# Two hand-overs in the query and key loop change places: when banks return to the queue, and when VectorE empties the transposes

## What is computed

```python
q = (rms_norm_2(q_lat, q_a_norm) @ w_qb).reshape(b, s, 8, 96)
kv = (rms_norm_2(kv_lat, kv_a_norm) @ w_kvb).reshape(b, s, 8, 128)
k_nope, v = kv[..., :64], kv[..., 64:]
k = jnp.concatenate([k_nope, k_pe], axis=-1)
q = rms_norm_2(q, q_norm)
k = rms_norm_2(k, k_norm)
q = jnp.concatenate([q[..., :64], apply_rope(q[..., 64:], pos)], axis=-1)
k = jnp.concatenate([k[..., :64], apply_rope(k[..., 64:], pos)], axis=-1)
# softmax(q k^T) v per block of 128 queries, causal
```

## Time and profile before

| | us |
|---|---|
| median of 3 runs | 1593.05 |
| lowest, highest | 1591.18, 1593.5 |
| the profiled execution | 1595.3 |
| its span, first to last instruction | 1593.5 |
| its mean granted TensorE clock | 0.967 of full |

### The profile page before, as it was taken

The page is one execution under the profiler, slowest core; times in us unless marked ns, Lnnn a source line. Parts: engine busy times, 40 slices in busy tenths (PEclk is TensorE's granted clock), DMA queues, the critical chain, the costliest instruction groups (busy, mean ns, idle before and its releaser), DMA issues.

```text
span 1593.5 us, 23667 instructions
## 1 busy us (share of the span) xinstructions
PE 1487.3 (93%) x10032; PEld 1152.6 (72%) x10032; DVE 799.6 (50%) x1257; ACT 585.6 (37%) x1017; POOL 312.2 (20%) x257
## 2 busy tenths in 40 slices
PE   5999898998899999999998999989899899998989
PEld 3777676876688888888876787767687577776667
DVE  7766785444533323324346555546643556454652
ACT  4256341445332222223323443334433343333531
POOL 0000233101011101100003323533300333343420
PEclk8999899998899999999989999999999999999999
DMA  9239243601132222232220122212122112111122
GB/s 362 73 109 110 89 175 132 214 29 51 57 102 95 93 93 93 97 132 95 93 94 30 61 69 67 64 42 67 53 93 100 40 53 80 53 67 53 53 69 90
DMA packets 51368, 143.11 MB, mean 90 GB/s; under 512 B 13248, under 2 KB 17984, under 8 KB 50496
## 3 DMA queue, kind: packets, MB, share of 16 engines
q1 hardware_dynamic: 51264, 141.60, 28.1%
HBM read 136.90 MB, written 4.69 MB: 89 GB/s over the span
## 4 chain that ended last, share of the span: by engine, by line
PE 80%; DVE 10%; ACT 4%; issue 3%; POOL 2%; DMA 1%; SPq 0%; DVEq 0%; POOLq 0%; ACTq 0%
PE b L407 78%; ACT arena L2207 3%; POOL arena L2867 2%; PE b L410 2%; DVE arena L1267 2%; DVE arena L1275 2%; DVE ringr L1267 1%; DVE arena L1973 1%; DVE arena L2164 1%; ACT ring L2210 1%; DVE arena L1271 1%; DMA cst<-in_cst 1%; DVE tile L1267 1%; DVE arena L1278 1%; POOL arena L2870 0%
## 5 line engine op out<-in xcount | busy, mean ns | idle before, releaser
L407 PE MATMUL b<-tile,ring 128*128 128x512 f32 (+1 forms) x1840 | 664.2, 400 | 8.3 <-ACT tile L2210 8.0
L407 PEld LDWEIGHTS b<-tile,ring 128*128 128x128 f32 (+1 forms) x1840 | 349.0, 190 | 95.6 <-issue 15.4
L407 PE MATMUL b<-HR,ring 128*128 128x512 f32 (+1 forms) x944 | 388.1, 411 | 24.1 <-DVE arena L1267 13.8
L1267 DVE TENSOR_TENSOR ringr<-ring,ring 128x1024 fp32r<-128x1024 f32 x186 | 240.6, 1298 | 317.0 <-ACT ring L2210 315.9
L407 PE MATMUL b<-HR,ringr 128*128 128x512 f32 (+1 forms) x944 | 373.4, 396 | 0.0
L407 PE MATMUL b<-arena 64*64 64x64 f32 (+10 forms) x3104 | 235.4, 279 | 34.8 <-DVE arena L1278 16.2
L2210 ACT ACTIVATE ring<-ring 128x1024 fp32r<-128x1024 f32 x186 | 195.3, 1054 | 163.2 <-DMA ring<-in_ws 163.2
L407 PEld LDWEIGHTS b<-HR,ring 128*128 128x128 f32 (+1 forms) x944 | 179.4, 190 | 73.2 <-issue 16.6
L407 PEld LDWEIGHTS b<-arena 64*64 64x64 f32 (+5 forms) x3104 | 149.3, 142 | 111.6 <-issue 87.7
L407 PEld LDWEIGHTS b<-HR,ringr 128*128 128x128 f32 (+1 forms) x944 | 179.4, 190 | 45.9
L407 PE MATMUL b<-tile,ringr 128*128 128x512 f32 x448 | 179.5, 401 | 0.0
(11 more groups left out here) (131 smaller groups left out, 1261.3 us busy)
## 6 DMA issues: line engine op xcount, KB each, us to landing
ring<-in_ws SPq DMA_DIRECT2D x218, 512.0 KB, 3.5
arena<-in_ws SPq DMA_DIRECT2D x15, 512.0 KB, 15.2
arena<-in_lw SPq DMA_DIRECT2D x2, 1280.0 KB, 6.0
X<-in_xT SPq DMA_DIRECT2D x2, 1024.0 KB, 6.2
arena<-scr_kpad SPq DMA_DIRECT2D x8, 256.0 KB, 11.4
X<-in_xT SPq DMA_DIRECT2D x1, 2048.0 KB, 11.6
outT<-X SPq DMA_DIRECT2D x8, 256.0 KB, 2.0
arena<-in_cst SPq DMA_DIRECT2D x1, 1088.0 KB, 6.0
```

Source lines behind the costliest of these rows:

```text
L407: return self.e.matmul(out, lhsT, rhs, start=start, stop=stop, skip_group_check=True)
L1267: return self.e.tensor_tensor(out=out, in0=a, in1=b, op=op)
```

## The change

TensorE's program gives the banks of queries and keys back after the transposes of the block before, instead of ahead of them. VectorE's program empties the transposes of the block before right after it has multiplied queries and keys, ahead of its wait for GpSimd and of the two instructions of the rotation.

```diff
 # Tensor.qk
             self.give((l, "v", q), (act, (l, "v", q)))
             yield
+            yield
+            if q:
+                transposes(q - 1)
             for hh in range(2):
                 self.give((l, "q", q, hh), (dve, (l, "q", q, hh)))
             self.give((l, "k", q), (dve, (l, "k", q)), (act, (l, "sqk", q)))
-            yield
-            if q:
-                transposes(q - 1)
             yield
 # Vector.qk
             self.tt(kq[:, 0, :, 0:64], h64(k.bank[l, "k", q]), bc(s_[:, 0], 64), ALU.mult).then_inc(*dve.inc((l, "k", q)))
             yield
+            if q:
+                transposes(q - 1)
             x1, x2 = kq[:, :, :, 64:80], kq[:, :, :, 80:96]
             self.wait_ge(pool, (l, "rot", q))
             self.tt(x1, k.T4[:, 0], k.T4[:, 1], ALU.subtract).then_inc(*dve.inc((l, "rot1", q)))
             self.tt(x2, k.T4[:, 2], k.T4[:, 3], ALU.add).then_inc(*dve.inc((l, "rot", q)))
-            if q:
-                transposes(q - 1)
             yield
```

## The result

The changed kernel took 1612.22 us (median of 4 runs, 1610.35 to 1612.73) against 1592.12 us before (median of 4, 1590.99 to 1593.5): a ratio of 1.0124 with a 95% interval from 1.0106 to 1.0141, slower by 20.1 us. The forecast was 1608.0, in a range from 1602 to 1613. The profiled execution is the fastest of the four, 1610.35 us with a span of 1608.6, 15.1 us more than the 1593.5 of before.

What follows compares the result with a forecast made beforehand. TensorE bounds the kernel, its six dense tiles waiting for VectorE's multiplications. Added stall 10.3 us plus clock 4.65 makes 14.95 on the profiled 1595.3, 1610.25; that execution lies 2.25 above the median, so 1608.0 us, range 1602 to 1613.

Steps and rivals of the forecast that it cites:

- What bounds: Dense tiles of blocks 1 to 3, both layers: TensorE waits 2.08 or 2.76 us for VectorE's first multiplication, on the path.
- Part 1, other banks: Dense tile gets the bank of a transpose instead of queries' first half, so it waits for VectorE's eviction.
- Part 2, 1.71 us a stall: Eviction follows the three multiplications, so each of six dense tiles starts 1.71 us later, 10.3 us in all.
- Part 3, the cover: Evictions fit VectorE's idle time before GpSimd's products end; rotation not later, split 1.4 us earlier, gain not passed on.
- Part 4, the clock: Longer stalls make all six dense tiles slow: three more clock drops of 1.55 us, 4.65 us.
- The bound of 2.6 us: Upper clock loss per dense tile, from the stretch after a 4.05 us idle time; 11 us more for all six.
- Sum: 10.3 + 4.65 = 14.95 us on the profiled execution, giving 1610.25 us; median expected at 1608.0 us.
- constant 2.25 us: How far the profiled execution lies above the median, used to go from 1610.25 to 1608.0 us.
- Only the stall: Rival: idle times before dense tiles grow, but clock drops no more often or costs little; 1603.4 us, 10%.
- Stretched evictions: Rival: GpSimd's products slow VectorE's evictions beside them, TensorE waits 1.4 us more six times; 1616.5 us, 4%.
- No change: Rival: weights, not the bank, end the dense tile's wait, so the bank wouldn't matter; 1593 us, 4%.
- faster: Rival: VectorE's queue delays the next block's sums, so earlier evictions gain up to 8.4 us; 1584.6 us, 2%.

Runs made afterwards that it cites:

- e7: Kernel before with the never-returned eighth bank given back to the queue at the start of the first hybrid layer: 1579.43 us, ratio 0.9927.
- e8: Kernel before with the eighth bank returned to the queue and VectorE's half of the change: 1572.66 us, ratio 0.9884.
- e1: Kernel before with TensorE's half of the change alone, VectorE's program left as it was: 1629.72 us, ratio 1.0239.
- e9: Changed kernel, both halves, with the eighth bank returned to the queue: 1572.31 us, ratio 0.9863 against the kernel before.
- e3: Kernel before with 8 useless matmuls put into each of the six TensorE stalls: 1589.45 us, ratio 0.9981.
- e4: Changed kernel with 14 useless matmuls put into each of the six TensorE stalls: 1600.77 us, ratio 1.004 against the kernel before.
- e2: Kernel before with VectorE's half of the change alone, banks given back as before: 1592.84 us, ratio 1.0001.
- the fillers: Useless matmuls put into the six stalls: 8 each in the kernel before, 1589.45 us; 14 each in the changed kernel, 1600.77 us.
- e5_after_again: Changed kernel unaltered, run again for a second profile: 1613.41 us, ratio 1.0138 against the kernel before.

## Why the prediction held, point by point

**What bounds.** Right. The six dense tiles stood on the path, and what released them was the first multiplication; taking that wait away gives 12.7 us (`e7`), and 19.5 with VectorE's half as well (`e8`).

**Part 1, other banks.** Right, and shown by `e1` and `e9`: the same order of give calls costs 36.8 us with VectorE's old order and 20.1 with its new one while there are seven banks, and nothing with eight and the new order.

**Part 2, 1.71 us a stall.** Right. Stalls of 3.79 and 4.48 us where 3.79 and 4.47 were worked out, 24.1 us in all for 24.1; 3.43 us for two between `e3` and `e4`.

**Part 3, the cover.** Right: the rotation still ends after GpSimd's products, nobody waits for the split, and `e2` is within 0.13% of the kernel before. What this part says of VectorE's gain, that it isn't passed on, holds only while TensorE stalls; `e7` and `e8` show it passed on once the stall is gone.

**Part 4, the clock.** This is the term that was mis-sized. That all six tiles would be slow was right, in both profiles. But 1.55 us was taken for each, and the two behind the 4.48 us stalls cost 2.5 to 2.8 us. The bound of 2.6 us had been worked out from the stretch behind the 4.05 us idle time and was put aside with the reason that the tiles are the same work. That reason failed: the same 24 matmuls last 7.2 or 8.4 us, by whether the clock falls inside the tile or is low already at its start. The term is 6.7 and 7.1 us in the profiles where 4.65 were forecast, and about 7.9 by the fillers. The length of the idle time alone doesn't give the price either: behind idle times of 6.87 us the tiles of `e1` cost 2.0 to 2.3 us, less than those behind 4.48. What else sets it stays open.

A second weak place is that the sum was made on one execution's share of drops and carried over to the median by a constant 2.25 us. The share changes from one execution to the next: `e2`, with the same stalls of TensorE, has two slow tiles in its profile (37.09 us for the six) where the kernel before had three. Whether a typical run of the kernel before pays 3.5 us of clock or 4.65 the medians can't say.

**Sum.** The median came out 4.2 us above the forecast 1608.0. For the profiled execution 1610.25 us were worked out and 1610.35 measured, and that close a hit is luck. Its stalls grew by 10.3 us and its tiles by 6.7, 2.1 more than forecast, but it reached the end of block 0's transposes, up to which the two programs do the same, 2.3 us earlier (848.37 for 850.66). Of the 20.1 us between the medians 10.3 are stall and 6.7 to 7.9 clock, together 17.0 to 18.2. The interval of the 20.1 us goes from 16.9 to 22.4, so the rest may be noise. Some 0.5 us of it shows in both profiles after, between the last dense tile of the first layer and the first stall of the second (355.26 and 355.45 us for 354.79); what it comes from wasn't traced.

**Rivals.** Only the stall: out, the clock's share grew by 6.7 us or more. Stretched evictions: out, 0.73 us beside GpSimd's products. No change and faster: out with these banks. The mechanism of the faster rival, VectorE's queue as the bound, turned up in `e7`, where its condition (no idle time ahead of the sums) is met.

## What to carry to other kernels

Where buffers are handed out first in, first out, the order of the give calls is a table of waits: before moving one, write down for every later take whose emptying it inherits, and what stands ahead of that in the emptying engine's queue. A consumer on the critical path should get the buffer that has been empty longest, and a buffer that was taken and never returned is worth looking for: here it was worth 12.7 us alone and 19.5 us together with the change's VectorE half. A stall on TensorE costs its own length and then some of the clock: here 1.5 to 2.8 us for each of the 18 stalls of 3.79 us or more.

## What was not expected of the hardware

The price of a clock drop is not one number, and it doesn't simply grow with the idle time. The same 24 matmuls last 5.67 us at full clock, 7.2 us behind those idle times of 2.08 to 3.80 us that brought the clock down, and 8.15 to 8.44 us behind 4.46 to 4.48 us (four cases). But in `e1_tensor_half` they last 7.67 to 7.98 us behind 6.86 and 6.87 us (four cases), and 8.30 and 8.48 behind 7.54 and 7.55. What goes with the price is where the clock fell. In all tiles of 7.2 us the first matmul takes 0.50 to 0.57 us, and the drop comes inside the tile; in all longer ones it takes 0.79 or 0.80 us, with the clock low from the start. In `e5_after_again`, where the tile began at 856.06 after 4.46 us idle, the clock was low over the first 14 of its 24 matmuls:

```profile
855.00:862.00 7.00, 5.94 (x14) 4.69 (x15) 3.56 (x6) 0.00 (x0) 2.64 (x4) 0.52 0.01 2
```

Matmuls of no use can pay: eight of them in each of six stalls made the kernel before 3.5 us faster (interval of the ratio 0.9969 to 0.9994).

Two VectorE instructions of two SBUF operands (the rotation) beside a GpSimd product lasted 1.84 us in `e7_bank8` and 2.22 in the earlier trace rows against 0.76, while evictions out of PSUM kept their length beside GpSimd's products. With the earlier trace rows this agrees with the Trainium skill, page "GPSIMD Engine Reference", section "Specifications", which names contention for VectorE instructions with two SBUF inputs, beside those in a 2-port perf mode.
